# Moving the arena of gated activations and mixed heads by 64 bytes in SBUF, to the address phase of the normed activations

## What is computed

```
h   = x + fox_mixer(rms_norm(x)) @ w_out
h   = h + (silu(gate) * val) @ w_down          gate, val = conv3(rms_norm(h) @ w_up)
h   = h + concat(gla(rms_norm(h)), dilated(rms_norm(h))) @ w_out_2
out = h + (silu(n @ w_gate) * (n @ w_up)) @ w_down_2       n = rms_norm(h)
```

## Time and profile before

| | |
|---|---|
| median of 3 runs | 2303.66 us (2303.3 to 2303.67) |
| the profiled execution | 2305.02 us, of which the span is 2303.1 us |
| granted TensorE clock, mean | 0.999 |
| TensorE busy | 2288.0 us, 99% |
| weight loads (PEld) busy | 1992.3 us, 87% |
| VectorE busy | 1623.7 us, 70% |
| ScalarE busy | 1235.2 us, 54% |
| HBM read | 418.98 MB, 184 GB/s over the span |

### The profile page before, as it was taken

The page is one execution under the profiler, slowest core; times in us unless marked ns, Lnnn a source line. Parts: engine busy times, 40 slices in busy tenths (PEclk is TensorE's granted clock), DMA queues, the critical chain, the costliest instruction groups (busy, mean ns, idle before and its releaser), DMA issues.

```text
span 2303.1 us, 39123 instructions
## 1 busy us (share of the span) xinstructions
PE 2288.0 (99%) x13190; PEld 1992.3 (87%) x13190; DVE 1623.7 (70%) x2378; ACT 1235.2 (54%) x1614; POOL 51.2 (2%) x78
## 2 busy tenths in 40 slices
PE   7999999999999999999999999999999999999999
PEld 6888888888888888888888888888888888888888
DVE  7777777788888888555567577767666766664554
ACT  6777765655555555444465577645444444443332
POOL 1111100000000000000000000000000000000000
PEclk9999999999999999999999999999999999999999
DMA  6555555555555555555545454555555555555553
GB/s 205 186 174 181 181 171 184 185 191 191 190 184 191 188 192 186 190 183 186 187 152 185 159 169 164 170 183 188 190 188 190 190 186 190 190 191 192 195 197 128
DMA packets 118593, 421.82 MB, mean 183 GB/s; under 512 B 13773, under 2 KB 15973, under 8 KB 118544
## 3 DMA queue, kind: packets, MB, share of 16 engines
q1 hardware_dynamic: 113760, 413.19, 54.0%
q0 software_dynamic: 2048, 5.39, 1.0%
q10 hardware_dynamic: 2736, 2.58, 0.3%
HBM read 418.98 MB, written 3.70 MB: 184 GB/s over the span
## 4 chain that ended last, share of the span: by engine, by line
PE 98%; DVE 1%; ACT 0%; DMA 0%; issue 0%; SPq 0%; DVEq 0%
PE acc L375 63%; PE acc L376 32%; PE b_score L430 0%; PE b_turn L435 0%; DMA xres<-xt 0%; PE b_mean L441 0%; PE b_mean L420 0%; PE b_mean L421 0%; PE b_val L427 0%; PE b_mean L442 0%; PE b_score L429 0%; PE b_mean L443 0%; ACT xs L852 0%; PE b_mean L513 0%; PE b_mean L510 0%
## 5 line engine op out<-in xcount | busy, mean ns | idle before, releaser
L375 PE MATMUL acc<-xs,whi 128*128 128x512 f32 x4344 | 1527.2, 395 | 2.2 <-DVE wlo L1048 1.8
L724 ACT ACTIVATE whi<-raw 128x1024 fp32r<-128x1024 f32 x783 | 828.4, 1062 | 853.7 <-PE acc L376 845.5
L1048 DVE TENSOR_TENSOR wlo<-raw,whi 128x1024 fp32r<-128x1024 f32 x783 | 959.6, 1229 | 394.7 <-ACT whi L724 392.9
L376 PE MATMUL acc<-xs,wlo 128*128 128x256 f32 x4344 | 1217.8, 280 | 0.0
L375 PEld LDWEIGHTS acc<-xs,whi 128*128 128x128 f32 x4344 | 814.2, 187 | 189.5 <-issue 5.1
L376 PEld LDWEIGHTS acc<-xs,wlo 128*128 128x128 f32 x4344 | 822.0, 189 | 1.7
L375 PE MATMUL acc<-hid,whi 128*128 128x512 f32 x1408 | 497.6, 397 | 0.0
L376 PE MATMUL acc<-hid,wlo 128*128 128x256 f32 x1408 | 395.6, 281 | 0.0
L1054 DVE TENSOR_REDUCE folded_t<-acc 128x256 f32<-128x512 f32 x336 | 231.8, 690 | 146.8 <-PE acc L376 136.7
L375 PEld LDWEIGHTS acc<-hid,whi 128*128 128x128 f32 x1408 | 264.7, 188 | 65.4
L376 PEld LDWEIGHTS acc<-hid,wlo 128*128 128x128 f32 x1408 | 264.3, 188 | 0.0
(11 more groups left out here) (190 smaller groups left out, 1000.9 us busy)
## 6 DMA issues: line engine op xcount, KB each, us to landing
raw<-wstream SPq DMA_DIRECT2D x783, 512.0 KB, 4.2
decay_row<-decay_scratch POOLq DMA_DIRECT2D x16, 128.0 KB, 3.6
out<-xres ACTq DMA_DIRECT2D x16, 128.0 KB, 3.5
xres<-xt SPq DMA_DIRECT2D x3, 512.0 KB, 8.8
dist_scratch<-bias_scratch POOLq DMA_DIRECT2D x8, 192.0 KB, 4.7
toeplitz<-dist_scratch POOLq DMA_DIRECT2D x8, 128.0 KB, 3.9
xres<-xt SPq DMA_DIRECT2D x2, 256.0 KB, 4.9
raw<-wstream SPq DMA_DIRECT2D x2, 256.0 KB, 5.7
```

Of the source, the lines that this page charges most:

```text
L375: pe.matmul(acc[bank_no][:, :], w_hi, x[:, kc, :, :].rearrange("p a s -> p (a s)"), start=first, stop=False)
L376: mm = pe.matmul(acc[bank_no][:, S:2 * S], w_lo, x[:, kc, 0, :], start=False, stop=last)
L724: act.activation(whi[slot][:, :], raw[slot][:, :], ACT.Copy).then_inc(hi_ready, 1)
L1048: dve.tensor_tensor(wlo[slot][:, :], raw[slot][:, :], whi[slot][:, :], ALU.subtract).then_inc(lo_ready, 1)
```

## The change

A name for the phase's modulus is added, xs's address is noted as it is allocated, and the arena begins at the next address that has the same remainder modulo 256 as xs. From sizes and addresses above that is 133,248 in place of 133,184: 64 bytes further. All that is in the arena moves by the same 64 bytes; nothing outside moves. The instructions, their order and their semaphores stay as they are.

```diff
--- before.py
+++ after.py
@@ -40,6 +40,7 @@
 FC = FF // P
 EPS = 1e-6
 BLOCKS = 8
+PHASE = 256
 UW = BLOCKS * P
 RING = 4
 AHEAD = 3
@@ -107,6 +108,7 @@
         whi = [sb(f"whi{i}", [P, UW], F32R) for i in range(RING)]
         wlo = [sb(f"wlo{i}", [P, UW], F32R) for i in range(RING)]
         xres = sb("xres", [P, KC, S])
+        xs_at = nc.sbuf_base
         xs = sb("xs", [P, KC, 2, S], F32R)
         folded_t = sb("folded_t", [P, S])
         vec = sb("vec", [P, VECTORS])
@@ -130,7 +132,7 @@
         hid = sb("hid", [P, S])
 
 
-        arena = nc.sbuf_base
+        arena = nc.sbuf_base + (xs_at - nc.sbuf_base) % PHASE
 
         def place(start):
             at = [start]
```

## The result

| | before | after |
|---|---|---|
| median | 2303.66 us | 2291.88 us |
| range of 5 runs | 2303.3 to 2304.17 | 2290.05 to 2293.03 |
| profiled execution (span) | 2305.02 (2303.1) | 2290.05 (2288.2) |

The ratio is 0.9948, with a 95% interval of 0.9933 to 0.9962: 11.8 us less, where 9.4 were forecast (2294.3 us). The profiled execution after is the shortest of its five, so the difference of the two spans, 14.9 us, overstates the gain.

The account below looks back on a forecast made before the run. TensorE, busy 99% of the span, was taken as the bound through its pace per matmul pair. Down stages gave -9.4 us, all else 0: 2303.66 - 9.4 = 2294.3 us; alone 2288.1 to 2297.2, the 8-in-10 range up to 2306.

Parts of the forecast that it names:

- the sum's one term: Down stages: 1408 pairs on hid2 get xs's good pace, 6.67 ns less each, 9.4 us gained; bounds 0 and 9.4.
- Projections, taken as 0, bounds 0 to 3.3: Output projections: pairs on mix may gain 3.3 us at most; taken as 0, after head_values, whose effect no row showed.
- Heads, taken as 0: Attention heads: between 1.9 us lost and 4.8 us gained over 22 heads; taken as 0.
- the bound of 4.8 us for all: Heads: if the scores leave the good pace, up to 33 pairs a head gain, 4.8 us in all.
- a head_mean that no longer turns the pace: Heads: 13 pairs after head_mean lose the good pace, 87 ns a head, 1.9 us over 22 heads.
- 1 us either way: The four GLA heads: taken as 0, with 1 us either way, an estimate of some 35 pairs a head changing pace.
- The phase is not the cause: Rival: hid2 and mix read slower for another reason of place; pace stays 353.3 ns, time 2303.7 us; chance 0.16.
- The up stage loses its good pace: Rival, at norm_mean: up stage turns slow, 9.3 us a layer, down stage gains nothing; 2322.3 or 2308.3 us; chance 0.13.
- no change: Up stages: no address that they read moves and both layers leave norm_mean at the good pace, so 0 us.
- hid2 settles slow though xs ended good: Rival, at the down stages' start: both layers slow, 2303.7 us (chance 0.03), or one of two, 2299.0 us (0.06).
- What would show it: Profile signs: 512-column matmuls on hid at 391 ns instead of 397, and xs rows of the up stages staying at 391.

Follow-up runs that it names:

- the run with hid2 alone: Only hid2 placed 64 bytes further, against the kernel before: 2294.68 us against 2304.35, ratio 0.9958.
- 256 bytes: The arena placed 256 bytes further, against the kernel before: 2304.58 us against 2304.35, ratio 1.0001.
- the run with hid2 and mix alone: The changed kernel with 192 bytes put behind mix, so the heads' buffers stand at their old remainders: 2323.38 us against 2304.73 for the kernel before.
- the repeat: The changed kernel itself, unaltered, timed again: 2293.37 us against 2304.73 for the kernel before, ratio 0.9952.
- the run with 128 bytes: The arena placed 128 bytes further, against the kernel before: 2301.95 us against 2304.73, ratio 0.9983.
- One program: The changed kernel with norm_mean's two matmul passes issued twice in the two up stages: eight executions from 2292.87 to 2321.24 us.

## Why the prediction was right, and where not

**The bound and the sum's one term.** TensorE's pace was the bound, and the down stages gave what was forecast: 9.4 us, measured as 4.7 and 4.7 in the profile and as 9.7 us in the run with hid2 alone. VectorE and DMA kept up: VectorE is busy 71% of the span, 70 before. The pace carried over from the last xs pair to hid in every profile where both stand at the weights' remainder, good as well as slow.

**Projections, taken as 0, bounds 0 to 3.3.** They gave 3.2 us in the first profiled execution and about half of that in the second. The row that I chose as nearest, the slow xs after the scores, was no guide: in the long run on mix behind head_values either pace comes out, from one execution to the next.

**Heads, taken as 0.** The fox heads gained 1.8 us, since the 24 pairs after the scores became good; the bound of 4.8 us for all was right in kind. The reverse, a head_mean that no longer turns the pace, happened in one head, the second dilated one:

```profile
L377 PE MATMUL acc<-xs,whi x14: 395/399/404, 1346.3 to 1350.9; 128*128 128x512 f32 x14
```

The four GLA heads lost 1.9 us, against "1 us either way": that bound was too narrow by half. The run with the GLA buffers put back shows the loss to hang on where they stand, and to be avoidable. The dilated heads gained 0.8, so layer 1's heads together lost 1.1 (1.2 by the table's rounded figures). The forecast missed 2.4 us of the medians' 11.8, and the projections and heads, both taken as 0, are where it lies: in the two profiled executions they give 3.9 and 2.6 us together.

**"The phase is not the cause" (0.16)** is refuted: 256 bytes do nothing, 64 do. With it goes, for this case, the conclusion from the 16-byte lines of the Trainium skill, SBUF — State Buffer, section "SBUF: two separate sides": hid2 at starts 64 bytes apart, both whole lines, ran at 346.7 and 353.3 ns a pair. The prediction's wording, that xs's phase itself allows the good pace, holds only while the weights stand there too: moved together, all keeps its pace.

**"The up stage loses its good pace" (0.13)** did not happen in ten timed executions of the changed kernel, but its outcome is real: three kernels near it show it, at the price worked out (9.3 us for an up stage, 14 us with its down stage). Its route is not borne out. It was to come when a good projection brings xs to norm_mean at the good pace; that happened in both layers of the changed kernel's first profile, and the up stages stayed good. All five slow up stages in the profiles came behind a slow projection. My reason against it, that norm_mean's own two matmuls may alone set what follows, is refuted by the run with hid2 and mix alone: the same two matmuls with the same operands, and both up stages slow. Nor does the pace ahead of them decide: from slow pairs it came out good (the repeat, layer 1) and slow (hid2 and mix alone). Which side a kernel falls on could not have been read from the trace. The forecast's "no change" for the up stages came true, but the reason that it leaned on is refuted, so that term, on which 9.3 us a layer and the down stages' gain hang, was right in part by luck.

**"hid2 settles slow though xs ended good" (0.09)** was not seen where xs and hid2 both stand at the weights' remainder. The nearest is the run with xs moved: hid2 at the weights' remainder, behind xs at 348.9 ns, settled slow.

**What would show it.** I named 391 ns on hid as the sign, and said that xs must stay at 391. Both now read 391 to 396 with a median of 394, at an unchanged pace for xs. The sign was wrong: the recorded length tells the pattern; the distance from start to start tells the pace.

**What stays open:** by what means the distance modulo 256 acts, why the place of the GLA buffers matters to the runs behind their small matmuls, and what exactly picks a pace where two are possible. That it can differ between executions, at fixed code and addresses, is shown by layer 1's projection in the two profiles of the changed kernel.

## What to carry to other kernels

Where TensorE is the bound, compare the start-to-start pace of equal matmuls by buffer and by stage; a difference of a per cent or two between buffers can be their distance to the weights modulo 256 bytes, and a few bytes of padding can give it back. But a long uninterrupted run keeps the pace that it begins with, so such an edit must be timed over several executions with all its stages looked at: padding in one place cost 18.7 us here, in stages whose buffers had not moved. Take the pace from start times, not from recorded lengths.

## What was not expected of the hardware

- A pair of 512- and 256-column matmuls settles in one of several regular patterns: even at 346.7 ns; 350 and 343 in turn, the same on average; 350, 361, 349, or even 353, both 353.3 on average; and 348.9 and 351.0 at other distances. At the weights' remainder 346.7 and 353.3 were seen, 64 past it 348.9 and 353.3, 128 off 351.0 alone, and 64 or 32 short of it 353.3 alone.
- The pace lasts through 1392 and then 704 pairs with a change of buffer between, if both stand at the weights' remainder, and through loop ends and semaphore waits that don't stall. Other matmuls between can change it, and so can a change to a buffer at another distance with none between. In the run with 128 bytes xs follows the slow hid directly and is good at once, 15 distances of 0.3467 us:

```profile
1153.33 0.40 PE L375 MATMUL acc<-hid,whi 128*128 128x512 f32 x1
1153.68 0.39 PE L375 MATMUL acc<-xs,whi 128*128 128x512 f32 x1
...
1158.88 0.40 PE L375 MATMUL acc<-xs,whi 128*128 128x512 f32 x1
```

- One program at full granted clock (0.999 to 1.0) gave 2293, 2307 and 2321 us in eight executions. The profiled one, of 2321 us, has all four long stages slow; the steps of 14 us between the groups fit one layer's price.
